# Layer 0 decode attention: value pages on 32 partitions in pieces of 8 KB

## What is computed

```
def gather_pages(pool, page_table):
    g = pool[page_table]
    return g.reshape((page_table.shape[0], page_table.shape[1] * pool.shape[1]) + pool.shape[2:])
...
    logits = jnp.einsum('bqhd,bkhd->bhqk', qi, k) * scale
    logits = logits + ci[..., :, None] - cum[:, :, None, :]
    p = masked_softmax(logits, mask)
    return jnp.einsum('bhqk,bkhd->bqhd', p.astype(v.dtype), v)
```

## Time and profile before

| what | value |
|---|---|
| time, median of 3 runs | 2514.32 us (2514.12 to 2522.76) |
| time of the profiled execution | 2519.72 us |
| its span, first to last instruction | 2518.0 us |
| mean granted TensorE clock | 0.91 of full speed |
| the stage of the change | 323 to 517 us of the span |
| PE busy over the span | 2126.2 us (84%) |
| bytes by DMA over the span | 322.05 MB |

### The profile page before, as it was taken

How to read it: one execution, slowest core, us unless ns; L and a number is a source line. 1 busy time by engine, 2 the same in 40 slices (tenths; PEclk the granted TensorE clock), 3 DMA queues, 4 the chain that set the end, 5 groups by cost and what they waited for, 6 DMA issues and landing times. The chain is left out here.

```text
span 2518.0 us, 48020 instructions
## 1 busy us (share of the span) xinstructions
PE 2126.2 (84%) x17829; PEld 1902.5 (76%) x17829; DVE 1208.7 (48%) x2282; ACT 578.4 (23%) x1074; POOL 265.1 (11%) x429
## 2 busy tenths in 40 slices
PE   4887746787999899698779996988977787999898
PEld 2873622375999899697469895988964487999898
DVE  4334711155444433434545657777743355444433
ACT  2220500012101000202136664444431212101000
POOL 0100233200000000000012222212223100000000
PEclk8997877887999999799779997999988898999999
DMA  8315189934323231223440003433448612232221
GB/s 345 117 51 233 36 315 386 380 111 134 92 83 92 86 103 47 62 76 118 195 144 2 1 2 102 127 108 108 122 169 294 226 59 84 85 90 84 93 92 59
DMA packets 237432, 322.05 MB, mean 128 GB/s; under 512 B 18235, under 2 KB 194440, under 8 KB 229807
## 3 DMA queue, kind: packets, MB, share of 16 engines
q1 hardware_dynamic: 215191, 239.29, 28.5%
q0 software_dynamic: 22048, 80.24, 9.1%
HBM read 311.56 MB, written 16.42 MB: 130 GB/s over the span
## 5 line engine op out<-in xcount | busy, mean ns | idle before, releaser
L441 PE MATMUL ps<-XHup,WHup 128*128 128x272 f32 x1408 | 293.4, 290 | 17.3 <-DVE XLup L415 13.7
L441 PE MATMUL ps<-XHup,WLup 128*128 128x272 f32 x1408 | 293.0, 290 | 0.0
L441 PE MATMUL ps<-XLup,WHup 128*128 128x272 f32 x1408 | 292.1, 289 | 0.0
L2168 PE MATMUL ps<-CHi,W1H 128*128 128x256 f32 x768 | 221.9, 289 | 38.0 <-DVE CLo L2271 38.0
L441 PEld LDWEIGHTS ps<-XHup,WHup 128*128 128x128 f32 x1408 | 223.1, 190 | 20.1 <-DVE XLup L415 14.5
L441 PEld LDWEIGHTS ps<-XLup,WHup 128*128 128x128 f32 x1408 | 223.0, 190 | 0.0
L441 PEld LDWEIGHTS ps<-XHup,WLup 128*128 128x128 f32 x1408 | 221.6, 190 | 0.0
L2169 PE MATMUL ps<-CLo,W1H 128*128 128x256 f32 x768 | 219.9, 286 | 0.0
L2170 PE MATMUL ps<-CHi,W1L 128*128 128x256 f32 x768 | 219.8, 286 | 0.0
L2168 PEld LDWEIGHTS ps<-CHi,W1H 128*128 128x128 f32 x768 | 150.2, 196 | 40.0 <-DVE CLo L2271 29.6
L434 DVE CAST WHup<-RAWup 128x1024 fp32r<-128x1024 f32 x88 | 61.1, 695 | 221.9 <-DMA RAWup<-in_w_up 163.7
(11 more groups left out here) (499 smaller groups left out, 4180.1 us busy)
## 6 DMA issues: line engine op xcount, KB each, us to landing
RAWup<-in_w_up SPq DMA_DIRECT2D x88, 512.0 KB, 3.8
Wearly<-in_w_mod SPq DMA_DIRECT2D x24, 1024.0 KB, 10.9
RAWdn<-in_w_down SPq DMA_DIRECT2D x14, 1408.0 KB, 6.1
KP<-in_cache_fox_k POOLq DMA_DIRECT2D x64, 256.0 KB, 6.0
KP<-in_cache_fox_k SPq DMA_DIRECT2D x64, 256.0 KB, 11.2
VP<-in_cache_fox_v POOLq DMA_DIRECT2D x64, 256.0 KB, 5.8
VP<-in_cache_fox_v SPq DMA_DIRECT2D x64, 256.0 KB, 11.4
RAWin<-in_nsa_w_in SPq DMA_DIRECT2D x20, 512.0 KB, 3.6
```

Source lines behind the costliest of these rows:

```text
L441: mm = self.nc.tensor.matmul(self.ps[:, banks + n, 0:HALF], w, x[:, n * HALF:(n + 1) * HALF], start=start, stop=stop)
L2168: nc.tensor.matmul(out, WH[:, sig, k, w], hi, start=(k == 0 and m == 0), stop=False, skip_group_check=True)
```

## The change

A page of values is read as 32 rows of four consecutive tokens (8 KB, contiguous in the cache) instead of 128 rows of one token. Page n goes to partitions 32*(n % 4) to 32*(n % 4)+31. So partition 32c + p of quarter a holds tokens 4p to 4p+3 of page 4a + c. The matmul number n of quarter a then takes token 4p + n of all four pages of the quarter in place of the whole page 4a + n, and the block of probabilities that it needs is every fourth column of PR, from column n on. The transpose therefore reads PR with a step of four elements. Everything else, keys included, stays; `key_place` and `value_place` only say where a page goes.

```diff
-        v_pages = i["cache_fox_v"][0].rearrange("n t h d -> n t (h d)")
+        v_pages = i["cache_fox_v"][0].rearrange("n (p t) h d -> n p (t h d)", t=PER)
+        ROWS = P // PER
...
-            KP, VP = sb("KP", [P, 2, PAGES, 512]), sb("VP", [P, 2, PAGES, 512])
+            KP, VP = sb("KP", [P, 2, PAGES, 512]), sb("VP", [P, 2, QUARTERS, PER, 512])
...
-                def pages(b, full, tile, rows):
+                def pages(b, full, rows, place):
                     for n in range(parity, PAGES, 2):
                         at = b * PAGES + n
                         page = engine.value_load(self.pages[0:1, at:at + 1], min_val=0, max_val=self.n_pages - 1)
-                        engine.dma_start(tile[:, b % 2, n, :], rows[ds(page, 1), :, :].rearrange("a p f -> p (a f)")).then_inc(full[b % 2], 16)
+                        engine.dma_start(place(n), rows[ds(page, 1), :, :].rearrange("a p f -> p (a f)")).then_inc(full[b % 2], 16)
+
+                def key_place(b):
+                    return lambda n: KP[:, b % 2, n, :]
+
+                def value_place(b):
+                    return lambda n: VP[n % PER * ROWS:(n % PER + 1) * ROWS, b % 2, n // PER, :, :].rearrange("p t f -> p (t f)")
...
-                            nc.tensor.transpose(ps[:, TURN, n * P:(n + 1) * P], PR[:, n * P:(n + 1) * P], self.ident)
+                            nc.tensor.transpose(ps[:, TURN, n * P:(n + 1) * P], PR[:, :].rearrange("p (x t) -> p t x", t=PER)[:, n, :], self.ident)
...
-                                                 VP[:, s, PER * a + n, :], start=(n == 0), stop=(n == PER - 1 and a > 0), skip_group_check=True)
+                                                 VP[:, s, a, n, :], start=(n == 0), stop=(n == PER - 1 and a > 0), skip_group_check=True)
```

More of the change, by code:

```diff
@@ L1607, in pages @@
                         page = engine.value_load(self.pages[0:1, at:at + 1], min_val=0, max_val=self.n_pages - 1)
-                        engine.dma_start(tile[:, b % 2, n, :], rows[ds(page, 1), :, :].rearrange("a p f -> p (a f)")).then_inc(full[b % 2], 16)
-                pages(0, k_full, KP, i["cache_fox_k"])
+                        engine.dma_start(place(n), rows[ds(page, 1), :, :].rearrange("a p f -> p (a f)")).then_inc(full[b % 2], 16)
[3 more added lines that the diff above has]
+                    return lambda n: VP[n % PER * ROWS:(n % PER + 1) * ROWS, b % 2, n // PER, :, :].rearrange("p t f -> p (t f)")
+                pages(0, k_full, i["cache_fox_k"], key_place(0))
                 for b in range(NB):
@@ L1614, in sequences @@
                             engine.wait_ge(scores, b)
-                        pages(b + 1, k_full, KP, i["cache_fox_k"])
+                        pages(b + 1, k_full, i["cache_fox_k"], key_place(b + 1))
                     if b >= 2:
                         engine.wait_ge(pv, b - 1)
-                    pages(b, v_full, VP, v_pages)
+                    pages(b, v_full, v_pages, value_place(b))
             with nc.Block(no_gpsimd_drain=True) as block:
```

## The result

| | before | after |
|---|---|---|
| time, median | 2517.16 us (2514.12 to 2522.76, 4 runs) | 2596.24 us (2589.76 to 2601.96, 4 runs) |
| span of the profiled execution | 2518.0 us | 2588.0 us |
| its time | 2519.72 us | 2589.76 us |

The change makes the kernel slower: ratio 1.0312, 95% interval 1.0287 to 1.0338, 79 us by the medians. The profiled execution of after is the fastest of its four, so the two profiles differ by only 70.0 us; the rest is not in a trace.

The account below looks back on a forecast made before the run. Key and value page transfers were taken to bound layer 0's decode attention. Landing +32.5 us, issue 0 and transposes 0 summed to +32.5: 2552 us against the profiled execution, 2547 against the median; range 2504 to 2590 us.

Parts of the forecast that it names:

- Value taken: Landing of value pages in layer 0's decode attention: every offset equally likely, factor 1.5, 119.9 us against 87.4, +32.5 us.
- the signs of being wrong: Closing list: no limit by quarters, worse than two quarters' worth, or 8 KB value pieces starving the other queue's key pieces.
- the engines in step: Rival for the value pages' landing: values at half rate, +72.4 us, 2587 us; 22%.
- The reading of MASK: MASK's load, 32 KB on 32 partitions, landed after 2.5 us beside SEL's 2.6: no penalty, but too little for a rate.
- nothing lost: Rival for the value pages' landing: engines' rows buffered or out of step enough, only the 7.5 us gain stays, 2507 us; 30%.
- The upper bound: Value pages' landing: if receiving goes by partitions, two quarters take 210 GB/s, values need 159.8 us, 72.4 us more.
- The estimate of +66.5 us: Value pages by the skill's port rule: about 218 GB/s for 8 of 16 ports, 153.9 us for the values.
- The gain per byte: Value pages in 8 KB rows at 420 GB/s instead of 384: 79.9 us for 87.4, 7.5 us less.
- Transposes: L1660's weight loads with a step of 16 bytes: 0 taken, 1.7 us for a sequence kept for the range.
- Issue: POOL's 1.14 us a page stays hidden with 2.6 us to spare, SP's instructions have no reason for more: 0.
- Buffers: Queue waits unmoved; late key pages lengthen PE's wait at L1639, so the price is the transfer time, once.
- Faster: Rival: long value rows speed key rows too, whole stage at 423 GB/s, -16.1 us, 2498 us; 10%.

Follow-up runs that it names:

- spread rows: Changed kernel with value rows still 32 pieces of 8 KB but on every fourth partition, PR written in matching order by ScalarE: 2510.69 us, ratio 0.9982; again 2510.55 us, 0.9973.
- a half for each queue: Changed kernel with SP issuing the value pages for partitions 0 to 63 and POOL those for 64 to 127, in place of even and odd pages: 2602.76 us.
- keys beside values: Changed kernel with all value pages issued by SP and all key pages by POOL: 2609.61 us.
- two DMAs to a page: Kernel with value rows on every fourth partition, each value page issued as two DMAs, one for partitions 0 to 63 and one for 64 to 127: 2567.61 us.
- 16 adjacent: Changed kernel with each value page as 16 pieces of 16 KB on 16 adjacent partitions, probabilities not reordered: 2682.50 us.

## Why the prediction was wrong

The direction and the place were right: the transfers set the stage, the loss arises where a page lands on 32 partitions, and it reaches the end of the program at full price. The number was wrong, and the range too, by 6 us at its upper end.

*The step that failed* is "Value taken", and with it the key rows, which the sum put at nothing. The step gave the values a factor of 1.5 on their 79.9 us (119.9 us), on the ground that nothing holds the engines in step, so that every offset is equally likely. How much time the engines spent on which rows can be added up from the packets of each trace, as the sizes tell value pieces from key rows (durations of all packets, divided by 16 engines; they overlap by some per cent):

| kernel, window in us | value pieces | key rows |
|---|---|---|
| before, 343 to 503.5 | 60.9 MB of both in 161.8 us, 377 GB/s | (same size) |
| spread rows, 343 to 495.5 | 33.5 MB in 81.6 us, 411 GB/s | 26.9 MB in 69.7 us, 385 GB/s |
| changed, 343 to 574 | 33.4 MB in 138.5 us, 241 GB/s | 28.1 MB in 93.4 us, 301 GB/s |
| a half for each queue, 343 to 590 | 33.6 MB in 140.2 us, 239 GB/s | 26.5 MB in 99.3 us, 266 GB/s |
| keys beside values, 343 to 597 | 31.0 MB in 132.6 us, 234 GB/s | 31.7 MB in 115.8 us, 273 GB/s |
| two DMAs to a page, 343 to 554 | 33.0 MB in 123.0 us, 268 GB/s | 26.7 MB in 86.4 us, 309 GB/s |
| 16 adjacent, 343 to 668 | 33.6 MB in 207.4 us, 162 GB/s | 27.0 MB in 111.3 us, 243 GB/s |

The values took 138.5 us, a factor of 1.73 on 79.9, where the step has 1.5. That is 19 us of the 38 by which the 70.6 us between the ends of the stage exceed the 32.5 of the sum. The other 19 us are the keys: at the 377 GB/s of before their 28.1 MB would have taken 74.6 us and not 93.4. The prediction has the keys' slowing only among the signs of being wrong, with no price.

The rival "the engines in step" named 272 GB/s for the stage and +72.4 us, and 269 and 70.6 were measured; the medians differ by 79. In part that is luck: it has the values at 210 GB/s (241 measured) and the keys unhurt. For values on 16 partitions full step would be a fourfold, and 162 GB/s is well above that quarter (105). So an offset between engines or queues may give something back, but much less than the step took. Three experiments offered it more room, and the times stayed at the changed kernel's or above it: a half for each queue (2603 us), 64 partitions (2598), keys beside values (2610). Even halves that alternate piece by piece left 2568. Why the engines can't fill the time of a narrow page with work for other receivers stays open, as the traces don't say which packet is of which engine.

*The reading of MASK* as "no penalty" told nothing, as the text itself feared. It was kept as 30% for "nothing lost".

*The upper bound* was taken by partitions, two quarters of four. The number fits by luck of the case; the reason was wrong. By that reason 64 partitions for each page would have been free (2598 us measured) and 32 spread ones as slow as 32 adjacent (2511). What fits all the runs is how many of the groups of four partitions that have a receiving lane of their own a DMA reaches.

The Trainium skill (SBUF — State Buffer, Door 1: The DMA port swizzle) has this rule: the port follows from bits 2 to 4 and bit 6 of the partition's number. The runs agree with it in their order: 32 adjacent (2596 us), 64 adjacent (2598), 32 of one half in steps of two (2599) and 16 in steps of eight (2604) all reach 8 of 16 ports by it, and steps of four (2511) all 16; 16 adjacent reach 4 and are the slowest (2683). The estimate of +66.5 us that the prediction worked out from its 218 GB/s came close to the profiles' 70.6, but for the values alone it is too high (153.9 us for the 138.5 measured), and it has nothing for the keys. The Trainium skill (SBUF — State Buffer, "Can I just issue two DMAs to hit both halves?") gives only 6% more for two concurrent DMAs, one on each half. No run here measures that figure, but with a half for each queue the values ran at 239 GB/s for 241, so nothing was gained there. I read the rule and gave its outcome 22%; the argument that outweighed it, the free offset, had no row behind it.

*The gain per byte* was right: reckoned at 7.5 us, 401 GB/s, and measured in the spread version at 401 GB/s, with medians 4.6 and 7.1 us below those beside them. In the changed kernel it is inside the loss.

*Transposes*: 0 taken, at most 1.7 us for a sequence. Measured 4 x 67 ns, 0.3 us. *Issue*: 0 taken, and POOL's instruction became 47 ns shorter, hidden. *Buffers*: the price was to be the transfer time, once; so it was. But it was to stand in PE's wait for keys, and only 31 of the 70 us do; as much stands in front of the value matmuls.

*Faster* (10%) had its condition, a mean above 414 GB/s, met by no version; with spread rows the stage stays at 401, value pieces at 411 and key rows, still 2 KB, at 385.

## What to carry to other kernels

Before a DMA's destination is narrowed, ask which groups of four partitions the one DMA reaches, rather than how many partitions, and don't count on other DMAs in flight to fill the rest: 32 rows on every fourth partition ran at full rate here (411 GB/s), 32 adjacent ones at 241. If longer pieces are wanted from a source of 32 rows, put the step into the destination and pay for the new order of tokens at a cheap place, here 0.5 us in ScalarE's write. Price what shares the queues and engines too: half of the miss lay in the key rows, which nobody had changed. And "nothing holds them together" is no ground for a midpoint between two bounds; where a rule with measured numbers stands against it, a value near the full price is likelier.

## What the runs showed that was not expected

Narrow transfers don't only take long, they slow down the others: with all keys in a queue of their own, key rows went at 232 GB/s for 380 while narrow value rows were under way, and PE's wait for keys rose to 172.8 us, from 37.7 before and 69.0 in the changed kernel. And the DMA share stayed between 1.00 and 1.03 in the stages at 246 to 401 GB/s, so it can't tell a slow receiver from a full one. Two engines' queues on the same 16 partitions (2658 us) were faster than on neighbouring groups of 16 (2683 us), in one execution each; the cause is open.
